# A decoder layer on one core: the order of the matmuls inside each block product of the MLP

## What is computed

```python
def ffn_sublayer(x, w_up, w_down, g_pre, g_post):
    h = rmsnorm(x, g_pre)
    a = jnp.square(jax.nn.relu(jnp.einsum('ntd,df->ntf', h, w_up)))
    return x + rmsnorm(jnp.einsum('ntf,fd->ntd', a, w_down), g_post)
```

## Time and profile before

| | us |
|---|---|
| time, median of 3 runs | 1964.88 (1962.88 to 1968.46) |
| time of the profiled execution | 1965.32 |
| its span, first to last instruction | 1963.6 |

### The profile page before, as it was taken

How to read it: one execution, slowest core, us unless ns; L and a number is a source line. 1 busy time by engine, 2 the same in 40 slices (tenths; PEclk the granted TensorE clock), 3 DMA queues, 4 the chain that set the end, 5 groups by cost and what they waited for, 6 DMA issues and landing times.

```text
span 1963.6 us, 38780 instructions
## 1 busy us (share of the span) xinstructions
PE 1922.8 (98%) x15210; PEld 1888.1 (96%) x15210; DVE 1318.1 (67%) x2014; ACT 1251.2 (64%) x1832; POOL 852.9 (43%) x625
## 2 busy tenths in 40 slices
PE   7999999999999999999999999999999999999998
PEld 7988899999989999999999999999999999999997
DVE  6566647222379777777777777776666666666686
ACT  6144424222277778777777777777777777777784
POOL 1000033111046566566666656545545544544572
PEclk9999999999999999999999999999999999999999
DMA  6422122522333555565565565975655556556542
GB/s 220 142 65 65 55 87 80 177 91 93 108 135 121 183 194 186 190 205 185 183 209 176 188 206 181 331 268 177 209 197 177 202 198 202 177 197 208 178 146 92
DMA packets 271756, 328.13 MB, mean 167 GB/s; under 512 B 8744, under 2 KB 237416, under 8 KB 270479
## 3 DMA queue, kind: packets, MB, share of 16 engines
q1 hardware_dynamic: 268208, 315.69, 48.7%
q10 hardware_dynamic: 3367, 9.96, 1.4%
HBM read 253.79 MB, written 74.22 MB: 167 GB/s over the span
## 4 chain that ended last, share of the span: by engine, by line
PE 92%; DVE 3%; DMA 2%; issue 1%; ACT 1%; SPq 0%; POOL 0%; DVEq 0%; ACTq 0%; POOLq 0%
PE banks L2258 22%; PE banks L1886 22%; PE banks L2259 21%; PE banks L2263 21%; PE banks L2214 1%; DMA mlp_kept<-mlp_rows 1%; PE banks L2191 1%; PE banks L1995 1%; PE banks L2026 1%; PE banks L2013 1%; PE banks L2280 1%; DVE w_lo L1291 0%; DMA w_raw<-in_w_in 0%; PE banks L1850 0%; DVE base L1650 0%
## 5 line engine op out<-in xcount | busy, mean ns | idle before, releaser
L2258 PE MATMUL banks<-mlp_part,splits 128*128 128x272 f32 x1792 | 467.4, 289 | 5.0 <-DVE y_sum L1688 4.4
L2259 PE MATMUL banks<-mlp_part,splits 128*128 128x272 f32 x1792 | 463.8, 286 | 0.0
L2258 PEld LDWEIGHTS banks<-mlp_part,splits 128*128 128x128 f32 x1792 | 335.6, 187 | 6.4 <-ACT splits L1173 3.9
L2259 PEld LDWEIGHTS banks<-mlp_part,splits 128*128 128x128 f32 x1792 | 336.7, 188 | 0.0
L1691 DVE TENSOR_TENSOR y_sum<-y_sum,banks 128x272 f32<-128x272 f32 x416 | 181.9, 437 | 180.0 <-PE banks L2263 180.0
L2263 PE MATMUL banks<-mlp_part,splits 128*128 128x272 f32 x1792 | 294.1, 286 | 0.0
L2258 PE MATMUL banks<-s_part,splits 128*128 128x272 f32 x960 | 248.5, 291 | 3.3 <-DVE quads L1688 3.3
L2263 PEld LDWEIGHTS banks<-mlp_part,splits 128*128 128x128 f32 x1792 | 250.2, 188 | 0.0
L938 ACT ACTIVATE w_hi<-w_raw 128x1024 fp32r<-128x1024 f32 x74 | 78.1, 1057 | 265.5 <-PE banks L1886 262.4
L2259 PE MATMUL banks<-s_part,splits 128*128 128x272 f32 x960 | 246.1, 288 | 0.0
L1886 PE MATMUL banks<-acts_hi,w_hi 128*128 128x272 f32 x1096 | 232.4, 293 | 11.7 <-DVE w_lo L1291 9.4
(11 more groups left out here) (273 smaller groups left out, 4311.1 us busy)
## 6 DMA issues: line engine op xcount, KB each, us to landing
raw_down<-in_w_down SPq DMA_DIRECT2D x128, 512.0 KB, 4.5
raw_up<-in_w_up SPq DMA_DIRECT2D x120, 512.0 KB, 6.7
mlp_part<-mlp_kept SPq DMA_DIRECT2D x56, 1088.0 KB, 8.3
mlp_kept<-mlp_hi SPq DMA_DIRECT2D x32, 952.0 KB, 4.5
w_raw<-in_w_in SPq DMA_DIRECT2D x40, 512.0 KB, 3.7
mlp_kept<-mlp_rows SPq DMA_DIRECT2D x32, 544.0 KB, 3.5
w_raw<-in_w_out SPq DMA_DIRECT2D x32, 512.0 KB, 3.4
mlp_kept<-mlp_rows SPq DMA_DIRECT2D x32, 408.0 KB, 2.6
```

The source lines that it names most:

```text
L2258: nc.tensor.matmul(out, wh, xh, start=first, stop=False, skip_group_check=not STARTS[i])
L2259: nc.tensor.matmul(out, wh, xl, start=False, stop=False, skip_group_check=not STARTS[i])
```

## The change

The three kinds of matmul are issued as three loops over j: all wh[j] xh[j], then all wh[j] xl[j], then, behind the same wait as before, all wl[j] xh[j]. The first matmul of the first loop starts the accumulation, as before. The number of matmuls, of weight loads and of waits stays.

```diff
-                for j in range(pairs):
-                    xh, xl = parts(j)
-                    wh = split_of(N, 0)[:, j, :]
-                    first = STARTS[i] and j == 0
-                    nc.tensor.matmul(out, wh, xh, start=first, stop=False, skip_group_check=not STARTS[i])
-                    nc.tensor.matmul(out, wh, xl, start=False, stop=False, skip_group_check=not STARTS[i])
+                for which in range(2):
+                    for j in range(pairs):
+                        nc.tensor.matmul(out, split_of(N, 0)[:, j, :], parts(j)[which], start=STARTS[i] and which + j == 0,
+                                         stop=False, skip_group_check=not STARTS[i])
                 pe.wait_ge(part_lo, N + 1)
                 for j in range(pairs):
                     xh, _ = parts(j)
```

## The result

The changed kernel takes 1969.55 us (median of 20 runs, 1966.79 to 1971.55) where the kernel before takes 1964.82 (20 runs, 1962.88 to 1970.42). The ratio over all runs is 1.0018, interval 1.0011 to 1.0025; the two medians alone give 1.0024. Forecast was 1956.4 with a range to 1966.0; the sign was wrong.

What follows compares the result with a forecast made beforehand. The prediction took TensorE, busy 98% of the span, to bound the kernel. Gains of 7.2 us down and 1.3 up sum to 8.5, so 1956.4 us against the median of 1964.88; the range was 1950 to 1966.

Steps and rivals of the forecast that it cites:

- What bounds the kernel: Whole kernel: TensorE, busy 98% of the span, sets the time in both projections; the distance between matmul starts is the cost.
- Costs put at nothing: Both projections: waits, end signal, repeated weight load coming later and later first read of the rest were costed at nothing.
- The up product: Up projection: sixteen matmuls go from 125.9 to 124.9 ns, 16 ns a product.
- The share that is given back up: Up projection: a longer stall at the sixth product takes back part; three products of seven keep their gain, 1.3 us.
- The room in the down projection: Down projection: ScalarE and VectorE wait for TensorE 0.38 and 0.46 us each; 17 ns fit into that thirty times.
- The term of down: Down projection: eight matmuls go from 125.1 to 123.0 ns, 16.8 ns a product, 7.2 us over 429 products.
- Half of it: Down projection: the run over the rest of the rows gains nothing, 3.6 instead of 7.2 us; 1960.0 us, chance 0.20.
- no change: Whole kernel: the 2 ns belong to the place in the product, not the order; 1964.9 us, chance 0.22 (given back included).
- Slower: Both projections: each of the eight down or sixteen up matmuls pays for a fresh weight tile, 130 ns; 1989.7 us, chance 0.08.
- The signs named ahead: Trace after: down period 1.476 to 1.485 us, up group 21.22, stall longer by 0.06; wrong if a new run's mean reaches 125.

Runs made afterwards that it cites:

- e1: Changed kernel's order of the rounded weight tiles alone, moving tiles ordered as in the kernel before (sums not the layer's); 1964.77 us, ratio 1.000.
- e11: Kernel before with the changed order in the up projection alone, down projection as before; 1963.30 us, ratio 0.9995.
- e13: Changed kernel, but each of eight down chunks reads its moving tiles in its own fixed step, 0 to 7 (sums not the layer's); 1964.45 us.
- e6: Changed order up; each of eight down chunks issues its eight matmuls with rounded weights in an order of its own; 1967.93 us.
- e2: Changed kernel's order of the moving tiles alone, rounded weight tiles in equal pairs as in the kernel before (sums not the layer's); 1969.37 us, ratio 1.002.
- e7: Kernel before, but up, VectorE copies the fourth product out of its bank ahead of the low part of the sixth's weights; 1966.76 us, ratio 1.0004.
- e8: Changed kernel with the same edit to VectorE's order as e7; 1968.64 us, ratio 1.0021.
- e9: Kernel before, but up, ScalarE makes the high copy of the sixth product's weights ahead of the rounding that waits for GpSimd's sums; 1960.22 us, ratio 0.9973.
- the snake: Kernel before, but down, rows (h) and rest (l) are read 0h 0l 1l 1h 2h 2l 3l 3h, then the weights' rest; 1963.72 us, ratio 0.9988.

## Why the prediction was wrong, point by point

**What bounds the kernel.** The down projection is TensorE's, as read. The up projection wasn't, though TensorE was busy for 590.00 of 590 us: the busy time of pipelined matmuls covers a stall of 0.18 us a group, and that stall was the sign of a loop through three other engines. The weight loads in the same row, 586.43 of 590 us against 570.00 of 570 in the down projection, did show a gap.

**Costs put at nothing.** Right: counts of matmuls and loads stay, e1 shows that the repeat of a weight tile saved nothing, and no wait arose from the later first read of the rest.

**The up product.** Right in sign and nearly in size: 16 ns forecast, 12 to 13 measured.

**The share that is given back up.** Wrong: three products of seven were to keep their gain, none did (e11), and the 1.3 us of the sum were 0. I had found the chain behind the stall and hung its beginning on the end of product 0, because VectorE's copy of that product is released by TensorE. But the step behind the copy, the relu, was held by GpSimd's instruction. The rows of GpSimd in the same window would have shown it. The room in the down projection was there, though 17 ns fit into waits of 0.38 and 0.46 us some twenty-five times, not thirty; it was not what failed.

**The term of down.** This step failed with its sign: -16.8 ns a product forecast, +13.3 measured (4480 to 4520 for three). I took the 123.0 ns of L2263's matmuls for a property of a straight run, and the unknown run's nearest row for a bound. e13 shows that a product of such runs over the rows' tiles alone does have 123.3. What failed is that a run's pace belongs to it: L2261 itself went from 492 to 504 ns when its neighbours changed, and e6 and e13 show that the whole repeated sequence of addresses sets the rhythm. The sequence of the changed kernel, even tiles, odd tiles, even tiles, has no row before, so its price lay open on both sides; the trace gave 119 to 130 ns for single distances and thus no reason to end the range at the pace of the interleaved part.

**Two rhythms.** The table of times had 1962.88 and 1968.46 for one kernel, and I read the difference as scatter. The trace of before had the quicker rhythm in the down stretch, which by the times about one execution in four doesn't have; the slower one stood in its last groups, behind 1893 us.

**The rivals.** "Half of it" fell, and "no change" too: the place in the product doesn't make the pace, since the last run went from 492 to 504 ns in its place. The Trainium skill's page "TensorE: Matmul & The Clock Gate", section "Back-to-back issue gap", gives an isolated gap by the number of columns alone (an estimate of 116 ns for 272); the runs have 123.3 to 126.7 for this one number, and the measurement decides. "Slower" came true in its place (down) and in its condition (three runs at a mean of 125.6 ns are near its 126.5), but its mechanism, a fresh weight tile, is refuted by e1 and e2, and its price of 24.8 us was five times too large. The loss, 0.18%, is inside what I called no change.

**The signs named ahead.** A period of 1.476 to 1.485 us: it was 1.507. Groups of 21.22: 21.27. A stall longer by 0.06 us: 0.08. The prediction was said to be wrong if a new run's mean reached 125, and it did.

## What to carry to other kernels

Where a stream of matmuls is the bound, a distance of one line is not a price that can be carried to another order: it is a part of the rhythm of the whole repeated sequence. Such orders are cheap to try, several in one execution by giving each stretch its own, and read by counting the matmuls in equal windows. Where an engine shows 98% and still stalls once in a group, look for a loop that doesn't pass through it before speeding it up: quicker products alone (e11) were worth nothing, an edit at another place (e7, e8) only moved the stall, and one instruction issued earlier (e9) gave 0.27%.

## What the runs showed of the hardware

The distance between two matmuls of 272 columns, at a full clock and with a load before each, depends on the order in which the moving tiles are read: in a fixed step over eight tiles 123.3 ns for 2176 bytes, 125.0 for 1088, 126.7 for 4352 (steps 2, 1 and 4 of e13), with the weights' order the same and the DMA share at 0.60 to 0.61. The order of the weight tiles has no effect that the runs show (e1: ratio 1.000, 0.9991 to 1.001).

Most sequences lock: for as long as nothing stalls the period is the same to 1 ns, in this kernel 4440, 4480, 4500, 4520, 4540 or 4560 ns for three products. Others repeat over two to five products (the snake alternates between 4467 and 4473, and the values 4510 and 4530 are such means). These periods lie on a grid: a product, or the few products after which a sequence repeats, takes a whole number of 6.67 ns, 222 to 228 of them for a product down, 450 (3000 ns) and 452 (3013) up. So the change cost two such units a product down and gained two up. Where the grid comes from, no run here shows.

One order can have two such periods, and it keeps the one that it has entered until the next stall. Each stall can change it: of 46 entries of the order of before 8 went to 4520, and the changed order always went to 4520 in the long stretch. What within the stall decides stays open.
